# Stick-breaking attention read in two parts a head, and another order of work at the first and the last stage of a two-block kernel

## The reference

```python
logits = jnp.einsum('bthd,bshd->bhts', q_blk, k).astype(jnp.float32) * scale
causal = key_pos[None, :] < q_pos[:, None]
log_beta = jax.nn.log_sigmoid(logits)
log_1mb = jnp.where(causal, jax.nn.log_sigmoid(-logits), 0.0)
tail = lax.cumsum(log_1mb, axis=3, reverse=True) - log_1mb
w = jnp.where(causal, jnp.exp(log_beta + tail), 0.0)
out = jnp.einsum('bhts,bshd->bthd', w.astype(v.dtype), v)
```

## Time and profile before

| | |
|---|---|
| median of 3 runs | 3036.1 us (3034.57 to 3037.15) |
| profiled execution | 3041.32 us |
| its span, first to last instruction | 3039.5 us |
| TensorE busy | 2931.4 us, 96% |
| VectorE busy | 1353.9 us, 45% |
| ScalarE busy | 1022.4 us, 34% |
| mean granted clock of TensorE | 0.990 of full speed |

### The profile page before, as it was taken

The page is one execution under the profiler, slowest core; times in us unless marked ns, Lnnn a source line. Parts: engine busy times, 40 slices in busy tenths (PEclk is TensorE's granted clock), DMA queues, the critical chain, the costliest instruction groups (busy, mean ns, idle before and its releaser), DMA issues.

```text
span 3039.5 us, 33999 instructions
## 1 busy us (share of the span) xinstructions
PE 2931.4 (96%) x14657; PEld 2428.8 (80%) x14657; DVE 1353.9 (45%) x1894; ACT 1022.4 (34%) x1324; POOL 77.4 (3%) x91
## 2 busy tenths in 40 slices
PE   7999999899999989999999999999999999999997
PEld 7878777787877878888876888888888886788886
DVE  4345246734623673323456443334433364644334
ACT  4322333432233333222445422224222254542222
POOL 0010000000000000000100000000000000000000
PEclk9999999899999999999999999999999999999999
DMA  5222112221221213222530323222322351223222
GB/s 210 72 97 78 62 57 82 96 82 70 79 88 37 89 60 115 97 97 97 100 102 25 111 97 111 97 97 97 109 100 97 111 99 56 79 88 111 97 97 83
DMA packets 41174, 275.89 MB, mean 91 GB/s; under 512 B 5492, under 2 KB 5682, under 8 KB 9792
## 3 DMA queue, kind: packets, MB, share of 16 engines
q1 hardware_dynamic: 35920, 254.82, 24.6%
q0 software_dynamic: 4288, 15.22, 2.5%
q10 hardware_dynamic: 816, 3.67, 0.3%
HBM read 269.50 MB, written 2.10 MB: 89 GB/s over the span
## 4 chain that ended last, share of the span: by engine, by line
PE 90%; DVE 5%; ACT 3%; issue 1%; DMA 1%; DVEq 0%; ACTq 0%
PE G L381 15%; PE G L382 15%; PE G L383 15%; PE G L393 11%; PE G L395 11%; PE G L394 11%; PE A L665 1%; PE A L882 1%; DVE w_lo L1477 1%; PE A L566 1%; PE A L904 1%; PE A L892 1%; PE A L680 1%; DMA x<-in_x 1%; PE A L655 1%
## 5 line engine op out<-in xcount | busy, mean ns | idle before, releaser
L381 PE MATMUL G<-xT_hi,w_hi 128*128 128x512 f32 (+1 forms) x2368 | 881.2, 372 | 16.3 <-DVE xT_lo L1518 6.0
L1477 DVE TENSOR_TENSOR w_lo<-raw,w_hi 128x2048 fp32r<-128x2048 f32 (+1 forms) x234 | 533.0, 2278 | 795.6 <-ACT w_hi L986 795.2
L383 PE MATMUL G<-xT_hi,w_lo 128*128 128x512 f32 (+1 forms) x2368 | 870.4, 368 | 0.0
L382 PE MATMUL G<-xT_lo,w_hi 128*128 128x512 f32 (+1 forms) x2368 | 869.9, 367 | 0.0
L986 ACT ACTIVATE w_hi<-raw 128x2048 fp32r<-128x2048 f32 (+1 forms) x234 | 443.7, 1896 | 963.2 <-PE G L395 523.1
L381 PEld LDWEIGHTS G<-xT_hi,w_hi 128*128 128x128 f32 x2368 | 449.1, 190 | 88.9 <-DVE xT_lo L1518 6.8
L383 PEld LDWEIGHTS G<-xT_hi,w_lo 128*128 128x128 f32 x2368 | 448.9, 190 | 73.2
L382 PEld LDWEIGHTS G<-xT_lo,w_hi 128*128 128x128 f32 x2368 | 449.5, 190 | 68.6
L393 PE MATMUL G<-w_hi,h_hi 128*128 128x512 f32 x704 | 274.6, 390 | 0.0
L395 PE MATMUL G<-w_hi,h_lo 128*128 128x512 f32 x704 | 274.0, 389 | 0.0
L394 PE MATMUL G<-w_lo,h_hi 128*128 128x512 f32 x704 | 273.9, 389 | 0.0
(11 more groups left out here) (287 smaller groups left out, 2963.0 us busy)
## 6 DMA issues: line engine op xcount, KB each, us to landing
raw<-in_stream SPq DMA_DIRECT2D x240, 1024.0 KB, 4.8
lnr<-in_ln_rows POOLq DMA_DIRECT2D x6, 1024.0 KB, 5.2
row<-in_rows POOLq DMA_DIRECT2D x6, 512.0 KB, 7.2
x<-in_x ACTq DMA_DIRECT2D x1, 2048.0 KB, 18.4
out<-x SPq DMA_DIRECT2D x4, 512.0 KB, 2.6
shift_t<-work POOLq DMA_DIRECT2D x32, 62.0 KB, 16.3
cst<-in_const ACTq DMA_DIRECT2D x1, 1474.0 KB, 22.9
cst<-in_const POOLq DMA_DIRECT2D x1, 1472.0 KB, 7.4
```

The costliest lines, as they stand in the source:

```text
L381: mm(o, a, hi[:, c, at:at + n], start=start and own_start, stop=False, **k)
L382: mm(o, a, lo[:, c, at:at + n], start=False, stop=False, **k)
L383: return mm(o, wl[:, col:col + P], hi[:, c, at:at + n], start=False, stop=stop, **k)
L1477: tt(w_lo[:, s, 0:nk, :], raw[:, r, 0:nk, :], w_hi[:, s, 0:nk, :].bitcast(F32), ALU.subtract).then_inc(lo_done, 1)
```

## The change

In `stick` the 1280 columns are handled in two parts, columns 512 to 1279 first and then 0 to 511, on all three engines. Each of the four semaphores counts twice a head. TensorE makes key blocks 1, 2, 3 and then 0. The gate's unit is cut in pieces of 3 matmuls: 7 after the logits and 3 after the sums for heads 1 to 3, and 2 in head 0 behind the last piece of the values. Before, it was 2 pieces of 12 after the logits, and 1, 0 and 1 such piece after the sums.

At the start, ScalarE's second weight split is moved behind the copies of the transposed memory. At the end, the last product has an order of its own, `FF_LAST_ORDER`, which finishes tile after tile. ScalarE no longer scales x. VectorE's `result` subtracts the mean and multiplies by the gain while ScalarE makes the inverse root, then scales and adds the offset, in the last tile by halves, which are stored apart. The other hunks hold the larger semaphore counts and the parameter `fine`.

```diff
...
                 else:
                     sp.dma_start(raw[:, s, :, :].rearrange("p k n -> p (k n)"),
                                  stream[b:b + 1].rearrange("o p n -> (o p) n")).then_inc(raw_in[s], 16)
-            for t in range(TILES):
-                sp.wait_ge(S["x_res"], 4 * (3 * DEPTH - 1) + t + 1)
-                sp.dma_start(out[0, t * P:t * P + P, :], x[:, t, :]).then_inc(out_done, 16)
-            sp.wait_ge(out_done, 16 * TILES)
+            parts = [(t, slice(0, D)) for t in range(3)] + [(3, slice(0, 512)), (3, slice(512, 1024))]
+            for i, (t, c) in enumerate(parts):
+                sp.wait_ge(S["x_res"], 4 * (3 * DEPTH - 1) + i + 1)
+                sp.dma_start(out[0, t * P:t * P + P, c], x[:, t, c]).then_inc(out_done, 16)
+            sp.wait_ge(out_done, 16 * len(parts))
         @block.tensor
...
             FF_ORDER = ((0, 0, 0, 4), (0, 1, 0, 4), (0, 2, 0, 4), (0, 3, 0, 4), (1, 0, 0, 4), (2, 0, 0, 2), (1, 1, 0, 4),
                         (2, 1, 0, 2), (1, 2, 0, 4), (1, 3, 0, 2), (1, 3, 2, 4), (2, 2, 0, 2), (2, 3, 0, 2))
+            FF_LAST_ORDER = ((0, 0, 0, 4), (0, 1, 0, 4), (1, 0, 0, 4), (2, 0, 0, 2), (1, 1, 0, 4), (2, 1, 0, 2), (0, 2, 0, 4),
+                             (1, 2, 0, 4), (2, 2, 0, 2), (0, 3, 0, 4), (1, 3, 0, 4), (2, 3, 0, 2))
             OUT_ORDER = ((0, 0, 0, 4), (0, 1, 0, 4), (1, 0, 0, 4), (1, 1, 0, 4), (0, 2, 0, 4), (0, 3, 0, 4), (1, 2, 0, 4),
                          (1, 3, 0, 4))
...
             def stick():
                 results_read()
-                values, gate = token_steps(), token_steps()
+                values, gate = token_steps(), token_steps(fine=True)
                 flat = A[:, :, :].rearrange("p b n -> p (b n)")
                 for h in range(HEADS):
                     if h:
-                        pe.wait_ge(S["s_w"], so_far(l, "s_w") + h)
-                    for i in range(4):
+                        pe.wait_ge(S["s_w"], so_far(l, "s_w") + 2 * h)
+                    for i in (1, 2, 3, 0):
                         n = (4 - i) * P
                         last = mm(flat[:, SB_AT[i]:SB_AT[i] + n], fB[:, h, i * P:i * P + P], fA[:, h, i * P:SEQ],
                                   start=(i != 3), stop=True, skip_group_check=True)
-                    last.then_inc(S["s_log"], 1)
+                        if i in (3, 0):
+                            last.then_inc(S["s_log"], 1)
                     advance(values, (5, 0, 0, 0)[h])
-                    advance(gate, (0, 2, 2, 2)[h])
-                    pe.wait_ge(S["s_sp"], so_far(l, "s_sp") + h + 1)
-                    for i in range(4):
+                    advance(gate, (0, 7, 7, 7)[h])
+                    for i in (1, 2, 3, 0):
+                        if i < 2:
+                            pe.wait_ge(S["s_sp"], so_far(l, "s_sp") + 2 * h + 2 - i)
                         for k in range(i, 4):
                             w, n = (k - i) * P, (4 - k) * P
                             mm(flat[:, SB_AT[i] + w:SB_AT[i] + w + n], c1v("minus_from" if k == i else "minus_ones"),
                                sB[:, SB_AT[k]:SB_AT[k] + n], start=False, stop=False, skip_group_check=True)
                         last = mm(flat[:, SB_AT[i]:SB_AT[i] + P], I, c1v("before_neg"), start=False, stop=True,
                                   skip_group_check=True)
-                    last.then_inc(S["s_cum"], 1)
+                        if i in (3, 0):
+                            last.then_inc(S["s_cum"], 1)
                     advance(values, (3, 0, 0, 0)[h])
-                    advance(gate, (0, 1, 0, 1)[h])
                     if h == 0:
                         finished(values)
+                    advance(gate, (2, 3, 3, 3)[h])
+                    if h == 0:
                         results_read()
-                    pe.wait_ge(S["s_w"], so_far(l, "s_w") + h + 1)
+                    pe.wait_ge(S["s_w"], so_far(l, "s_w") + 2 * h + 2)
                     if h:
                         pe.wait_ge(S["s_pvu"], so_far(l, "s_pvu") + h)
                     for j in range(4):
...
-                        gemm_last_half(downs, FF_ORDER, h_hi, h_lo, between, True)
+                        gemm_last_half(downs, FF_ORDER if L < 3 * DEPTH - 1 else FF_LAST_ORDER, h_hi, h_lo, between, True)
...
             def layer_norm(L):
                 inner, ahead = L < 3 * DEPTH - 1, L % 3 != 1
-                if inner and ahead:
+                if not inner:
+                    for t in range(TILES):
+                        rsqrt(1, t, preload=False)
+                    Pos.u += 1
+                    return
...
             def stick():
                 act.preload_act_table_set(LN_EXP)
-                flat = A[:, :, :].rearrange("p b n -> p (b n)")[:, 0:1280]
+                flat = A[:, :, :].rearrange("p b n -> p (b n)")
+                parts = (slice(512, 1280), slice(0, 512))
                 for h in range(HEADS):
                     if h == 3:
                         split()
-                    act.wait_ge(S["s_log"], so_far(l, "s_log") + h + 1)
-                    link(fn(sB[:, 0:1280], flat, ACT.Abs))
-                    link(fn(sB[:, 0:1280], sB[:, 0:1280], ACT.Exp, scale=-1.0))
-                    fn(sB[:, 0:1280], sB[:, 0:1280], ACT.Ln, bias=1.0).then_inc(S["s_ln"], 1)
+                    for i, c in enumerate(parts):
+                        act.wait_ge(S["s_log"], so_far(l, "s_log") + 2 * h + i + 1)
+                        link(fn(sB[:, c], flat[:, c], ACT.Abs))
+                        link(fn(sB[:, c], sB[:, c], ACT.Exp, scale=-1.0))
+                        fn(sB[:, c], sB[:, c], ACT.Ln, bias=1.0).then_inc(S["s_ln"], 1)
                     if h == 0:
                         split()
-                    act.wait_ge(S["s_cum"], so_far(l, "s_cum") + h + 1)
-                    fn(sA[:, 0:1280], flat, ACT.Exp).then_inc(S["s_w"], 1)
+                    for i, c in enumerate(parts):
+                        act.wait_ge(S["s_cum"], so_far(l, "s_cum") + 2 * h + i + 1)
+                        fn(sA[:, c], flat[:, c], ACT.Exp).then_inc(S["s_w"], 1)
                     if h == 0:
                         evac4(lambda b: tA[:, b, :])()
                         split()
...
                         fn(xn[:, t, :], mem_t[:, t, :], ACT.Square, accum_out=rs_v[:, 8 + t:9 + t]).then_inc(S["m_square"], 1)
                     rsqrt(2, 8, preload=False)
                     split()
-                    split()
                     tr_hi(xT_hi, 2, 2, 2)
+                    split()
                     act.wait_ge(x_loaded, 16)
                     for t in range(TILES):
                         if t:
...
             SB_AT = (0, 512, 1024, 896)
             def stick():
-                flat = A[:, :, :].rearrange("p b n -> p (b n)")[:, 0:1280]
-                E = sB[:, 0:1280]
+                flat = A[:, :, :].rearrange("p b n -> p (b n)")
+                parts = (slice(512, 1280), slice(0, 512))
                 for h in range(HEADS):
                     if h == 3:
                         split()
-                    dve.wait_ge(S["s_ln"], so_far(l, "s_ln") + h + 1)
-                    link(stt(out=E, in0=flat, scalar=0.0, in1=E, op0=ALU.max, op1=ALU.add))
-                    for i in range(4):
-                        e = sB[:, SB_AT[i]:SB_AT[i] + P]
-                        ins = tt(e, e, c1v("before"), ALU.mult)
-                    ins.then_inc(S["s_sp"], 1)
+                    for n, c in enumerate(parts):
+                        dve.wait_ge(S["s_ln"], so_far(l, "s_ln") + 2 * h + n + 1)
+                        link(stt(out=sB[:, c], in0=flat[:, c], scalar=0.0, in1=sB[:, c], op0=ALU.max, op1=ALU.add))
+                        for i in ((1, 2, 3), (0,))[n]:
+                            e = sB[:, SB_AT[i]:SB_AT[i] + P]
+                            ins = tt(e, e, c1v("before"), ALU.mult)
+                        ins.then_inc(S["s_sp"], 1)
                     if h == 0:
                         split()
                     dve.wait_ge(S["s_pv"], so_far(l, "s_pv") + h + 1)
...
             def residual(L, t):
                 param(dve, L // 3, "ln_in", L % 3 + 1, 3)
-                if L < 3 * DEPTH - 1:
-                    dve.wait_ge(S["tp"], 8 * L + 4 * (t // 2) + 4)
+                dve.wait_ge(S["tp"], 8 * L + 4 * (t // 2) + 4)
                 dve.wait_ge(S["ln_z"], 4 * L + t + 1)
                 link(tt(x[:, t, :], x[:, t, :], lnr[:, 0, :], ALU.mult))
                 tt(x[:, t, :], x[:, t, :], lnr[:, 1, :], ALU.add).then_inc(S["x_res"], 1)
+            def result(t, parts):
+                link(stt(out=x[:, t, :], in0=x[:, t, :], scalar=mean_var[:, t, 0:1], in1=lnr[:, 0, :],
+                         op0=ALU.subtract, op1=ALU.mult))
+                newton(1, t)
+                for c in parts:
+                    stt(out=x[:, t, c], in0=x[:, t, c], scalar=rs_r[:, t:t + 1], in1=lnr[:, 1, c],
+                        op0=ALU.mult, op1=ALU.add).then_inc(S["x_res"], 1)
```

(85 more changed lines are left out.)

10 lines of the change are left out of this document (5 added, 5 removed).

## The result

| | before | with the change |
|---|---|---|
| median | 3036.53 us (3034.57 to 3037.15, 4 runs) | 3020.98 us (3018.64 to 3023.87, 4 runs) |
| ratio, 95% interval | | 0.995 (0.9934 to 0.9965) |
| profiled execution: time, span | 3041.32, 3039.5 us | 3023.87, 3022.1 us |

The change makes the kernel 15.6 us faster by the medians and 17.4 us by the spans of the two profiled executions. 3018.5 us was forecast. In a later comparison of the same two kernels (`changed_again`) the changed one took 3018.89 us (3017.06 to 3019.95, 5 runs) against 3037.68 us (median of 10 runs), a ratio of 0.9938 (0.9925 to 0.995). One of those ten runs of the kernel before was a slow one, with 3310.61 us at a mean granted clock of 0.845, and the ratio leaves it out.

A forecast was written before the change was run, and what follows sets the result against it. TensorE, busy 96% of the span, was taken as the bound, so only its idle time or the ends could be won. 12.4 + 6.7 - 1.5 = 17.6 us off 3036.1 gave 3018.5 us, range 3013.5 to 3025.5.

The forecast's parts named there:

- Stick, 12.4 us less: In `stick`, both layers: TensorE's waits for softplus, last exponential and head 0's values end, 12.4 us less.
- The waits that I named: In `stick`, per layer: three for the masked softplus, one for head 2's last exponential, one for head 0's values.
- the spare time of both parts: In `stick`: the first part lies ready 1.1 us before TensorE asks, the second 2.7 us.
- The restart of 0.1 us: In `stick`: products behind a wait take 0.1 us more, 2.42 against 2.32 us, counted as gained with each wait.
- The end, 6.7 us less: Last product to last store: VectorE finishes tile 3 6.2 us sooner, and the halved last store saves 0.5 us.
- The new wait: In the last product: TensorE waits 0.9 us for block 1's low part, 1.0 with restart.
- VectorE's time a tile: At the end, in `result`: 5.1 us a tile, with the first pass covering the root's idle time.
- The halved store: Last store at half size: saves between 0 and 1.3 us, taken as 0.5 us.
- The start, 1.5 us more: Memory keys to second product: TensorE's gap grows to 4.1 us and its clock falls, costing 1.5 us, between 0 and 2.4.
- the first rival: At the start: the clock doesn't fall in the 4.1 us gap, time 3017.0 us; chance 0.20.
- The sum: Whole kernel: 12.4 + 6.7 - 1.5 = 17.6 us less, from 3036.1 to 3018.5 us.

The follow-up runs named there:

- undone_filled: Changed kernel with ScalarE's start as before and six unread identity products in TensorE's gap between memory keys and values; 3017.70 us, ratio 0.9935 to the kernel before.
- gap_filled: Changed kernel with 18 unread identity products in TensorE's gap between memory keys and values; 3016.40 us, ratio 0.9933 to the kernel before.
- start_only: Kernel before with only ScalarE's second weight split moved behind the copies of the transposed memory; 3037.83 us, ratio 1.0003.
- end_only: Kernel before with only the end changed: tile by tile last product, VectorE's pass during the root, last store in halves; 3029.76 us, ratio 0.998.

## Why the prediction was right

- **Stick, 12.4 us less**: right in mechanism and size. It measured 12.5 us (2 x 6.26). The waits that I named are the ones that ended, each half's share came out as expected ahead of its run from the same durations (84.4 and 88.0 us, measured 84.36 and 87.89), and the spare time of both parts was off by 0.2 us at most. The restart of 0.1 us behind each wait belongs in such a sum: the brackets of the earlier trace rows alone come to 10.1 us. Where the text ahead of the prediction says that four semaphores count twice a head, it is five.
- **The end, 6.7 us less**: 6.3 us. The new wait (0.98 us), VectorE's time a tile (5.05 us from 2996.75 to 3001.80, 5.1 forecast), and TensorE as the last to come were as worked out. The term was 0.4 us too large. VectorE reads the last tile 29.7 us behind its addition of the first half, where the times forecast give 29.4 (3025.2 less 2995.76), and takes 5.3 us for it in place of 5.1: the passes were taken at 1.25 us and took 1.28, and the two halves take 1.41. The profile of before had a pass of this form, with a value per partition as an operand, that could have been read: `x<-fA,rs_r,x` over 1024 columns, 1.28 us against 1.22 for `x<-x,lnr`. The halved store was taken at 0.5 us, and its landing fell by 0.6, from 2.6 to 2.0 us. The Trainium skill (DMA: Bandwidth & Descriptors, Anatomy of one DMA) gives a fixed and a variable part for transfers that GpSimd issues. The estimate worked out from it was 3.2 and 2.6 us. These stores are issued by SyncE, and both land 0.6 us sooner than that, while the difference agrees.
- **The start, 1.5 us more**: the step that was only half right. It took the keys to be slow for as long as before, hence a gap of 4.1 us and a fall of the clock. In the profiled execution the keys were fast, the gap was 5.37 us, and the start cost 1.8 us, which is 2.3 us of low clock less 0.5 us because x landed earlier. In two other executions with this start the keys were slow for longer, the gap was 2.9 us, and nothing fell: that is the first rival, which had a chance of 0.20. That the profile of the changed kernel came close to the 1.5 us is luck. The price depends on the execution, and the medians don't tell it from nothing. That x sets the start of the second product, and no edit moves it, was right: it starts 10.9 us behind the first square of x in every profile but that of `undone_filled`, old start or new.
- **The sum**: by the spans 17.4 us less, made of +1.8, -12.5 and -6.3, and -0.4 in the stretches between, which the change doesn't touch. The first comparison gave 15.6 us by the medians, the second 18.8. That both are within 2 us of the 17.6 is as much as whole times can say; the stretches carry the account. Most of the spread of the whole times lies in the stretches that the change doesn't touch. From the end of layer 1's stick to VectorE's addition at the end it took 2035.1 us before, 2035.5 in the changed kernel, 2030.0 in `gap_filled` and 2029.9 in `start_only`, with the same instructions. The middle of the fourteen profiles is 2032.3, so 2.8 of the 5.2 us by which the profiled execution of before lay above its median can be placed here. The windows of this stretch, before and in `start_only`:

```profile
961.00:2980.00 2019.00, 1980.10 (x9703) 1630.63 (x9702) 885.15 (x1224) 691.60 (x902) 43.69 (x54) 0.99 0.29 94
```

```profile
961.00:2980.00 2019.00, 1979.78 (x9727) 1631.42 (x9726) 885.05 (x1223) 691.24 (x902) 43.65 (x54) 1.00 0.29 94
```

More matmuls fit in the same time where the clock was up. One of the places is 1592 to 1600, with a granted clock of 0.82 before and 1.00 in `start_only`:

```profile
1592.00:1600.00 8.00, 6.34 (x20) 2.79 (x19) 3.82 (x9) 3.07 (x7) 0.00 (x0) 0.82 0.38 132
```

```profile
1592.00:1600.00 8.00, 6.29 (x27) 3.37 (x26) 4.98 (x17) 3.83 (x11) 0.00 (x0) 1.00 0.40 132
```

The records of the granted clock in the fourteen traces put a size to it. In this stretch the clock is at its lower level for 13.7 us in the three profiles of 2029.9 to 2030.0 us, for 20.5 us in the seven of 2032.0 to 2032.5, for 23.9 us in the two of 2033.2 and 2033.5, and for 27.3 us in the two of 2035.1 and 2035.5. That is 0.39 us for each microsecond at the lower level, somewhat less than the 0.44 us that the prediction worked out for an engine without idle time. So the clock accounts for the 5 us, though no run changed it by itself. Whole times show the same: of the eleven runs of `start_only`, two took 3034.7 and 3034.8 us at a mean granted clock of 0.993, five 3036.2 to 3037.9 at 0.992, three 3040.2 to 3040.5 at 0.991, and one 3043.4 at 0.989. The changed kernel had 0.991 to 0.994 in its first comparison (median 3020.98 us) and 0.993 to 0.994 in its second (3018.89).

The lowest median is that of the changed kernel with its gap filled, 3016.4 us. Its interval overlaps those of the changed kernel.

## What to carry to other kernels

Where an engine waits at the end of a chain of passes over other engines, cut the chain at the dependence that the data really has, put the part that asks for less first, and deal the filler work so that each question falls behind its answer. Both are needed, and each can be worked out to a few tenths of a microsecond from two durations of each pass. Read an effect of a microsecond in a kernel of three milliseconds from a stretch of the trace between two fixed instructions, not from the whole time, and look at the granted clock of each run before two whole times are compared. A product that is moved ahead of a wait that it doesn't end gains nothing, and lengthens the idle gap in front of that wait.

## What the hardware showed that I had not expected

- The clock fell 1.3 us behind an idle gap of 2.30 us (`end_only`, from 36.84 on), with nine matmuls 0.12 us apart in between. It stayed up behind gaps of 2.88 and 2.91 us (`start_only`, `changed_again`). The length of one gap does not decide it, and the fall can come when the work has begun again.
- The keys' product ran at 2.4 GHz from its start behind an idle gap of 2.05 us in the changed kernel, and at 1.2 GHz at first behind gaps of 2.05 us in `changed_again` and 2.06 in `start_only`. Ahead of it stood only transposes in each of them. In `gap_filled` it began 0.12 us apart behind a gap of 2.44 us and was 0.21 us apart from 18.31 on.
- A stretch of 2030 us with the same instructions took up to 5.6 us more in one execution than in another, and the time that the granted clock spent at its lower level in it (13.7 to 27.3 us) goes with it.
